# A modulation prologue in which every second unit is split into a high and a low part

## The reference

```python
sh1, sc1, g1, sh2, sc2, g2 = split(silu(c) @ mod_w[0] + mod_b[0])          # 1024 -> 6 x 1024
csh1, csc1, ...            = split(silu(c_ctx) @ mod_w[0] + mod_b[0])
n_lat = rmsnorm(x, norm1_g[0]) * (1 + sc1) + sh1
n_ctx = rmsnorm(ctx, norm1_g[0]) * (1 + csc1) + csh1
q, k, v, xr, gr = split(n_lat @ w_in);  kc, vc, xc = parts of n_ctx @ w_in
```

## Time and profile before

| | |
|---|---|
| median of 3 runs | 2468.14 us |
| profiled execution | 2467.85 us, its span 2466.0 us |
| TensorE busy | 98% of the span |
| first matmul of the projection | 57.85 us after the span's start |
| modulation units on TensorE | 15.55 to 53.7 us |
| granted clock of TensorE, whole span | 0.995 |

### The profile page before, as it was taken

How to read it: one execution, slowest core, us unless ns; L and a number is a source line. 1 busy time by engine, 2 the same in 40 slices (tenths; PEclk the granted TensorE clock), 3 DMA queues, 4 the chain that set the end, 5 groups by cost and what they waited for, 6 DMA issues and landing times.

```text
span 2466.0 us, 29290 instructions
## 1 busy us (share of the span) xinstructions
PE 2416.2 (98%) x11158; PEld 1982.8 (80%) x11158; DVE 1109.6 (45%) x1427; ACT 513.3 (21%) x816; POOL 1052.4 (43%) x507
## 2 busy tenths in 40 slices
PE   8999999989999999999999999999999999999998
PEld 3888878878788888888887888887788888888886
DVE  5677848844634443422224644346422222222224
ACT  4544438851200000000002200002200000000003
POOL 3333347888533334444334243553344433333340
PEclk9999999999999999999999999999999999999999
DMA  9444465533332233211111111111111111111111
GB/s 307 151 149 158 148 165 99 104 112 103 120 119 101 95 119 119 85 48 46 43 51 43 35 52 43 55 53 46 52 52 51 43 44 49 43 43 50 51 43 69
DMA packets 223343, 207.08 MB, mean 84 GB/s; under 512 B 40135, under 2 KB 193443, under 8 KB 222755
## 3 DMA queue, kind: packets, MB, share of 16 engines
q1 hardware_dynamic: 216787, 187.16, 25.8%
q10 hardware_dynamic: 5904, 16.78, 1.9%
q0 software_dynamic: 576, 2.10, 0.2%
HBM read 185.73 MB, written 20.28 MB: 84 GB/s over the span
## 4 chain that ended last, share of the span: by engine, by line
PE 92%; DVE 4%; ACT 2%; issue 1%; POOL 0%; DMA 0%; SPq 0%; DVEq 0%; POOLq 0%; ACTq 0%
PE bank L798 28%; PE bank L800 28%; PE bank L799 28%; PE bank L911 1%; DVE probs L1976 1%; PE bank L1041 1%; PE bank L1067 1%; PE bank L1066 1%; DVE bank L1663 1%; PE bank L1028 1%; PE bank L832 1%; ACT probs L1502 1%; PE bank L1029 1%; DVE act_lo L1669 1%; DMA mod_ring<-in_mod_w 0%
## 5 line engine op out<-in xcount | busy, mean ns | idle before, releaser
L628 POOL TENSOR_TENSOR w_hi<-raw,ones 128x1024 fp32r<-128x1024 f32 x184 | 359.6, 1954 | 1185.0 <-PE bank L800 1132.0
L798 PE MATMUL bank<-act_hi,w_hi 128*128 128x512 f32 x2160 | 844.7, 391 | 8.5 <-DVE hid_f L2026 5.8
L799 PE MATMUL bank<-act_hi,w_lo 128*128 128x512 f32 x2168 | 846.5, 390 | 0.0
L800 PE MATMUL bank<-act_lo,w_hi 128*128 128x512 f32 x2160 | 843.2, 390 | 0.0
L798 PEld LDWEIGHTS bank<-act_hi,w_hi 128*128 128x128 f32 x2160 | 406.9, 188 | 93.8 <-DVE hid_f L2026 6.6
L799 PEld LDWEIGHTS bank<-act_hi,w_lo 128*128 128x128 f32 x2168 | 408.7, 189 | 84.6
L800 PEld LDWEIGHTS bank<-act_lo,w_hi 128*128 128x128 f32 x2160 | 406.9, 188 | 85.5
L631 POOL TENSOR_TENSOR w_lo<-raw,w_hi 128x1024 fp32r<-128x1024 f32 x184 | 468.4, 2546 | 14.5
L1686 DVE SCALAR_TENSOR_TENSOR h<-bank,mods,h 128x512 f32<-128x512 f32 x432 | 319.0, 748 | 243.7 <-PE bank L800 243.0
L2026 DVE TENSOR_TENSOR hid_f<-silu_g,bank 128x512 f32<-128x512 f32 x86 | 59.1, 687 | 689.7 <-PE bank L800 687.4
L798 PE MATMUL bank<-hid_hi,w_hi 128*128 128x512 f32 x704 | 276.0, 392 | 1.6 <-DVE hid_lo L2033 1.4
(11 more groups left out here) (232 smaller groups left out, 2328.5 us busy)
## 6 DMA issues: line engine op xcount, KB each, us to landing
raw<-in_ffn_w_gu SPq DMA_DIRECT2D x88, 512.0 KB, 3.8
mod_in_f<-in_mod_w SPq DMA_DIRECT2D x48, 512.0 KB, 4.7
raw<-in_ffn_w_down SPq DMA_DIRECT2D x44, 512.0 KB, 3.6
mod_in_p<-in_mod_w SPq DMA_DIRECT2D x32, 512.0 KB, 6.6
raw<-in_o_w_in SPq DMA_DIRECT2D x24, 512.0 KB, 3.7
raw<-in_e_w_in SPq DMA_DIRECT2D x20, 512.0 KB, 5.1
mod_ring<-in_mod_w SPq DMA_DIRECT2D x16, 512.0 KB, 9.4
raw<-in_e_w_out SPq DMA_DIRECT2D x16, 512.0 KB, 3.6
```

The source lines that it names most:

```text
L628: nc.gpsimd.tensor_tensor(w_hi, raw[:, parity, :], ones[:, 0:1].to_broadcast([P, UNIT]), ALU.mult).then_inc(s_hi, 1)
L798: pe.matmul(dst, w_hi, x_hi, start=first, stop=False)
L799: pe.matmul(dst, w_lo, x_hi, start=False, stop=False)
L800: return pe.matmul(dst, w_hi, x_lo, start=False, stop=last)
```

## The change

- Odd modulation units (1, 3, ..., 15) are no longer multiplied in fp32. ACT rounds each to fp32r (`mod_high`) into slot 2 or 3 of `w_hi4`, POOL subtracts (`mod_low`) into the same slot of `w_lo4`, and TensorE multiplies both parts with `cond_r`.
- `cond_r` has four columns: the high parts of silu(c) and silu(c_ctx), and their low parts. The even units use `cond4`, with two columns of zeros. The sums therefore have four rows; the transposes have four columns, and VectorE adds the two extra ones.
- Unit 0 comes after row tile 5 (before: 4), so five units stand among the tiles, and the spreads come after unit 8 (before: 9).
- Weight units 2 and 3 are loaded behind all modulation units, and POOL makes the weight splits behind all eight `mod_low`.
- ACT has the roundings of units 1 and 3 behind the squares of tiles 6 and 8, that of 5 behind the root, those of 7 and 9 behind Exp, those of 11, 13 and 15 behind the mod_row copies of sh1.

```diff
+        def mod_slot(u):
+            return 2 + u // 2 % 2
...
@@ sync
             for u in range(8, 2 * FT):
                 load_first_mod(u)
-                if u in (11, 13):
-                    j = (u - 7) // 2
-                    load_unit(j, j % 2, column_unit(w_in, order_p[j]))
+            for j in (2, 3):
+                load_unit(j, j % 2, column_unit(w_in, order_p[j]))
...
@@ gpsimd
+            nc.gpsimd.memset(cond4[:, :, 2:4], 0.0)
...
+            def mod_low(u):
+                pool.wait_ge(s_mhi, u // 2 + 1)
+                nc.gpsimd.tensor_tensor(w_lo4[:, mod_slot(u), :], mod_ring[:, u % 8, :], w_hi4[:, mod_slot(u), :],
+                                        ALU.subtract).then_inc(s_mlo, 1)
+
+            for u in range(1, 2 * FT, 2):
+                mod_low(u)
             for j in range(4):
-                split(j, j, j % 2)
+                split(j, j, j % 2, None if j < 2 else (s_modmm, 2 * FT))
...
@@ tensor
             def first_mod(u):
                 c, k = divmod(u, FT)
-                pe.wait_ge(s_mod[u % 8], 16 * (u // 8 + 1))
+                if u % 2:
+                    pe.wait_ge(s_mlo, u // 2 + 1)
+                else:
+                    pe.wait_ge(s_mod[u % 8], 16 * (u // 8 + 1))
                 for a in range(2):
-                    mm = pe.matmul(bank[0:2, 4 + 2 * c + a, :], cond[:, k, :], mod_ring[:, u % 8, a * HALF:(a + 1) * HALF],
-                                   start=(k == 0), stop=(k == FT - 1))
+                    dst, cols_ = bank[0:4, 4 + 2 * c + a, :], slice(a * HALF, (a + 1) * HALF)
+                    if u % 2:
+                        pe.matmul(dst, cond_r[:, k, :], w_hi4[:, mod_slot(u), cols_], start=False, stop=False)
+                        mm = pe.matmul(dst, cond_r[:, k, :], w_lo4[:, mod_slot(u), cols_], start=False, stop=(k == FT - 1))
+                    else:
+                        mm = pe.matmul(dst, cond4[:, k, :], mod_ring[:, u % 8, cols_], start=(k == 0), stop=False)
...
-                if tt >= 4:
-                    if tt == 4:
+                if tt >= 5:
+                    if tt == 5:
                         pe.wait_ge(s_cond, 2)
+                        pe.wait_ge(s_condl, 1)
                         pe.wait_ge(s_param, 2)
-                    first_mod(tt - 4)
+                    first_mod(tt - 5)
             pe.wait_ge(s_xp, TT + CT)
-            for u in range(TT + CT - 4, 2 * FT):
+            for u in range(TT + CT - 5, 2 * FT):
                 first_mod(u)
-                if u == 9:
+                if u == 8:
                     pe.wait_ge(s_rstd, 1)
...
@@ scalar
+            def mod_high(u):
+                act.wait_ge(s_mod[u % 8], 16 * (u // 8 + 1))
+                if u >= 4:
+                    act.wait_ge(s_modmm, u - 3)
+                nc.scalar.copy(w_hi4[:, mod_slot(u), :], mod_ring[:, u % 8, :]).then_inc(s_mhi, 1)
...
+                    act.wait_ge(s_cond, 2)
+                    nc.scalar.copy(cond_r[:, :, 0:2], cond4[:, :, 0:2]).then_inc(s_condh, 1)
+                    nc.scalar.copy(cond[:], cond4[:, :, 0:2]).then_inc(s_cond, 1)
...
+                if tt in (6, 8):
+                    mod_high(tt - 5)
...
+            mod_high(5)
             act.wait_ge(s_xinv, 1)
             act.wait_ge(s_turn, TT + CT)
...
+            mod_high(7)
+            mod_high(9)
             for c in range(2):
                 act.wait_ge(s_modmm, FT * (c + 1))
...
+                if c == 0:
+                    for u in (11, 13, 15):
+                        mod_high(u)
...
@@ vector
-                    V.tensor_tensor(dst[:, c, :], summed[:, :, j], mod_bias[:, c, :], ALU.add).then_inc(s_modset, 1)
+                    V.tensor_tensor(dst[:, c, :], summed[:, :, j], mod_bias[:, c, :], ALU.add).then_inc(s_modadd, 1)
+                dve.wait_ge(s_modadd, 2 * (c + 1))
+                for j, dst in enumerate((mods, mods_ctx)):
+                    V.tensor_tensor(dst[:, c, :], summed[:, :, 2 + j], dst[:, c, :], ALU.add).then_inc(s_modset, 1)
...
+                if tt == 4:
+                    dve.wait_ge(s_condh, 1)
+                    dve.wait_ge(s_cond, 3)
+                    V.tensor_tensor(cond_r[:, :, 2:4], cond4[:, :, 0:2], cond_r[:, :, 0:2], ALU.subtract).then_inc(s_condl, 1)
```

More of the change, by code:

```diff
@@ L153, in backbone @@
         ctx_t = at(72, "ctx_t", [P, FT, CTX])
-        mod_row = at(83, "mod_row", [2, 2, UNIT])
+        mod_row = at(83, "mod_row", [4, 2, UNIT])
         x_sq = at(92, "x_sq", [P, D])
@@ L158, in backbone @@
         b_rows = at(80.5, "b_rows", [96, P])
+        cond4 = at(81, "cond4", [P, FT, 4])
+        cond_r = at(81.25, "cond_r", [P, FT, 4], F32R)
         far_rows = at(96, "far_rows", [P, HEADS * NR * GRID * GRID // (4 * P)])
@@ L242, in backbone @@
         s_modrow_d = sem("mod_row_by_dve")
+        s_condh, s_condl, s_mhi, s_mlo, s_modadd = (sem("cond_hi"), sem("cond_lo"), sem("mod_unit_hi"), sem("mod_unit_lo"),
+                                                    sem("mod_bias_added"))
         s_mu = (sem("mod_unit_landed0"), sem("mod_unit_landed1"))
@@ L925, in mod_turn @@
                 for m in range(FT):
-                    mm = pe.transpose(bank[:, 3, 2 * (c * FT + m):2 * (c * FT + m) + 2], mod_row[:, c, m * P:(m + 1) * P],
-                                      ident[0:2, 0:2])
+                    mm = pe.transpose(bank[:, 3, 4 * (c * FT + m):4 * (c * FT + m) + 4], mod_row[:, c, m * P:(m + 1) * P],
+                                      ident[0:4, 0:4])
                 mm.then_inc(s_modt, 1)
@@ L1386, in _ @@
                     for j in range(2):
-                        nc.scalar.activation(cond[:, :, j], par[:, PAR["c"] + j * FT:PAR["c"] + (j + 1) * FT], ACT.Silu).then_inc(s_cond, 1)
+                        nc.scalar.activation(cond4[:, :, j], par[:, PAR["c"] + j * FT:PAR["c"] + (j + 1) * FT], ACT.Silu).then_inc(s_cond, 1)
+                    act.wait_ge(s_cond, 2)
+                    nc.scalar.copy(cond_r[:, :, 0:2], cond4[:, :, 0:2]).then_inc(s_condh, 1)
+                    nc.scalar.copy(cond[:], cond4[:, :, 0:2]).then_inc(s_cond, 1)
                 act.wait_ge(s_x[tt], 16)
@@ L1404, in _ @@
                 for a in range(2 - c):
-                    nc.scalar.copy(mod_row[:, c, a * HALF:(a + 1) * HALF], bank[0:2, 4 + 2 * c + a, :]).then_inc(s_modrow, 1)
+                    nc.scalar.copy(mod_row[:, c, a * HALF:(a + 1) * HALF], bank[0:4, 4 + 2 * c + a, :]).then_inc(s_modrow, 1)
+                if c == 0:
+                    for u in (11, 13, 15):
+                        mod_high(u)
             act.wait_ge(s_xp, TT)
@@ L1782, in mod_first @@
                 dve.wait_ge(s_modt, c + 1)
-                summed = bank[:, 3, 2 * c * FT:2 * (c + 1) * FT].rearrange("p (m j) -> p m j", j=2)
+                summed = bank[:, 3, 4 * c * FT:4 * (c + 1) * FT].rearrange("p (m j) -> p m j", j=4)
                 for j, dst in enumerate((mods, mods_ctx)):
-                    V.tensor_tensor(dst[:, c, :], summed[:, :, j], mod_bias[:, c, :], ALU.add).then_inc(s_modset, 1)
+                    V.tensor_tensor(dst[:, c, :], summed[:, :, j], mod_bias[:, c, :], ALU.add).then_inc(s_modadd, 1)
+                dve.wait_ge(s_modadd, 2 * (c + 1))
+                for j, dst in enumerate((mods, mods_ctx)):
+                    V.tensor_tensor(dst[:, c, :], summed[:, :, 2 + j], dst[:, c, :], ALU.add).then_inc(s_modset, 1)
             for s, credits in ((s_conv, 1), (s_lru, 1), (s_macc, 2), (s_hup, 2),
@@ L1816, in _ @@
             dve.wait_ge(s_modmm, 2 * FT)
-            V.tensor_copy(mod_row[:, 1, HALF:UNIT], bank[0:2, 7, :]).then_inc(s_modrow_d, 1)
+            V.tensor_copy(mod_row[:, 1, HALF:UNIT], bank[0:4, 7, :]).then_inc(s_modrow_d, 1)
             mod_first(1)
```

## The result

The changed kernel took 2481.54 us (median of 4 runs, 2480.77 to 2482.45); the kernel before, run beside it on the same chip, 2467.94 (2467.33 to 2468.61). The ratio is 1.0056, 95% interval 1.0045 to 1.0068: 13.6 us slower. The profiled execution took 2480.77 us, its span is 2478.9.

What follows compares the result with a forecast made beforehand. TensorE, busy 98% of the span, was taken to bound the kernel, so the prologue's end decides. Terms A to D, 2.8 + 2.35 + 8 + 1 = 14.2 us, on 2467.85 gave 2482 us, range 2473 to 2489.

Steps and rivals of the forecast that it cites:

- term A: Modulation prologue: the wait for unit 7 and the low clock delay x_rms, so gains come 2.8 us later.
- Term B: Around VectorE's gains: the low part of unit 1 falls between the two gains operations, +2.35 us.
- Term C: Modulation of rows: splits of weight units 2 and 3 collide with VectorE's first eight act_lo, +8 us (0 to 8.5).
- Term D: Projection: TensorE, fed in pieces, starts its second group at the low clock, +1 us (0 to 2.5).
- Part 1: Odd units on TensorE: four fp32r matmuls of 0.23 us replace four fp32 records, 6.6 us less work.
- Part 2: Waits of odd units in the prologue: landing, ACT's rounding, POOL's subtraction; TensorE stands 5.5 us before unit 7.
- Part 3: Weight splits moved later on POOL: they and VectorE's SBUF-only operations exclude each other; x_rms is free.
- Edits costed at nothing: Copies of cond and a small subtraction are hidden; SP's moved queue has 10 us cover for gates and for weights.
- Nothing waits: Rival: the 6.6 us come in full as unit 7's low part is ready by 32.7; 2461 us, chance 0.07.
- The wait at unit 7 alone: Rival: only term A, without VectorE and POOL excluding each other; 2470.7 us, chance 0.09.
- SP's queue too late: Rival: the strip is slower by more than its cover, 5 us more, 2487 us; chance 0.05.
- Half the collisions: Rival: weight units 2 and 3 land late behind the spill, fewer collisions; 2473 to 2477 us, chance 0.17.

Runs made afterwards that it cites:

- experiment 1: The changed kernel with ACT rounding modulation unit 7 before its wait for VectorE's reciprocal; 2474.88 us, ratio 1.0028.
- 11: The changed kernel with weight units 2 and 3 split behind all act_lo, ACT's sp wait moved, far rows and memsets brought forward; 2473.92 us.
- 6: The changed kernel with unit 7 rounded earlier, weight unit 0 split behind it, weight units 2 and 3 behind all act_lo, ACT's sp wait moved; 2471.46 us.
- pair 3 and 4: The changed kernel with all 16 modulation units in fp32; splits of weight units 2 and 3 behind the modulation matmuls, 2470.52 us, or free, 2465.95 us.
- experiment 2: The changed kernel with POOL splitting weight units 2 and 3 only behind all 24 act_lo; 2482.11 us, ratio 1.0059.
- 5: The changed kernel with weight units 2 and 3 split behind all act_lo and ACT's sp wait moved to just before first use; 2480.47 us.
- experiment 8: The changed kernel with ACT issuing the 4 MB spill of h after the first eight act_hi; 2481.77 us, ratio 1.0055.
- experiment 7: The changed kernel with only units 9, 11, 13, 15 split, weight unit 0 first, weight units 2 and 3 behind all act_lo, sp wait moved; 2469.78 us.

## Why the prediction was right

The forecast was 2482.0 in a range of 2473 to 2489; it came to 2481.5. The two causes are the two that it named, and each was taken away by itself (experiments 1 and 11: 6.3 and 7.1 us, together 13.4 of 13.6; they were not taken away together with all eight units kept, except in 6, which had the late queue). Inside the second, one place and one wait were wrong, and part of the closeness of the total is luck: on the span, term A came to 3.9 us where 2.8 was said, B to 2.2 for 2.35, C to 5.0 for 8 and D to 1.4 for 1, so C was 3 us too large and A and D 1.5 us too small.

**Part 1, the work removed.** Right. Steps of 0.23 us as taken from the earlier trace rows; the even units and the small additions on VectorE cost what they did.

**Part 2 and term A (+2.8, bounds +0.6 and +4).** The chain was right link by link: x_diag 30.53, table load 33.58, unit 7's rounding behind it on ACT, POOL's low part, TensorE's stall of 4.7 us (5.5 was said), the low clock behind it. ACT's row in the changed kernel, to be laid beside the earlier trace rows:

```profile
30.53 3.03 ACT L1431 ACTIVATE x_diag<-ident,x_std 128x128 f32<-128x128 f32 x10 [3.90 <-DVE x_std L1848]
33.58 1.28 ACT L1434 ACT_TABLE_LOAD   x1
```

The term measured +3.9, the upper bound: all of unit 8 ran at the low clock (3.57 us for four records, twice 1.8), so that the spread began at 43.8 and not at 42.8. The mis-sized part is the length of that low stretch, and it changes from one execution to the next: experiments 2, 5, 8 and 11 have the same program up to there, and their gains came at 58.73, 56.83, 58.20 and 60.08 us, 1.4 to 4.6 us behind the kernel before; unit 8 took 3.07, 2.55 and 3.58 us in the first three. So +2.8 was a fair middle, and +3.9 is one profile's. Unit 0 at 2.4 GHz with a longer stall behind it (3.14 us) was the alternative that the text gave, at no other cost.

**Part 3.** That VectorE and POOL exclude each other was right, and shown by the pair 3 and 4, where nothing else differs. The rows give it as an exchange one for one: from 71 us on, four of VectorE's operations each end 0.3 to 0.6 us behind one of POOL's four (two act_lo end at 76.49, POOL's second operation at 75.95). x_rms, which has one input in PSUM, loses nothing: 16 take 11.52 us beside POOL's low parts and splits (11.51 in the earlier trace rows). By the rule in the Trainium skill ("SBUF — State Buffer", Who interferes with whom) a VectorE operation with one SBUF input, outside the two-port modes, does not meet GpSimd, and one with two does. The trace agrees: 11.52 us beside POOL for x_rms, and 5.20 in place of 1.40 for two act_lo. Shared bandwidth would not make 2.2 us of a 128x8 operation.

**Term B (+2.35).** The sum was right, +2.2 (6.05 less 3.86), its place was not: the low part of unit 1 (59.70 to 62.04) met the two `scaled` behind the gains, and did not fall between the two gains operations.

**Term C (+8, bounds 0 and 8.5).** VectorE lost 7.2 us (its last ctx_lo is 13.24 us late, 6.05 of it from before), so the price held. The step that failed is "landing 5 us and more after issue ... are split while VectorE makes the first eight act_lo". The first of them landed 13.1 us after issue, and the collision fell on the second eight. The bound of 0 for that case was wrong: it took the splits behind the eighth act_lo to be free, and TensorE needed the second eight as well as the chain behind them. Of VectorE's 7.2 us TensorE felt 2.9 (78.5 to 81.3) and 2.1 (95.4 to 97.5). The second is a link that the prediction did not have: the chain of 23 small operations, ACT's wait for them and the bank that ACT frees, with 0.8 us of cover before. Experiment 8 shows what the forecast's own placing would have given: the same total.

**Term D (+1).** The low clock came in a later group and cost 1.7 us (4.0 x 0.42), inside its bounds of 0 to 2.5. The first group's low stretch was shorter than before, 10 matmuls and not 12, which gives back 0.3: the second group starts at 71.64 in place of 65.88, 5.76 us late and not 6.05. On the span: 3.9 + 2.2 - 0.3 + 2.9 + 1.7 + 2.1 = 12.5 of the 12.9 us; the remaining 0.4 comes after the sixth group and has no single place.

**Edits costed at nothing.** SP's queue brought no stall: its cover was to be 10 us and TensorE's delay of 13 us lengthened it. The condition was stated ("gone if terms A to D were zero") and experiments 5 to 7 are that case, though by another way: not the transfers came too late, but POOL's splits moved onto VectorE's recurrence. There it cost 5.1 us (experiment 7); that the text gave 4 to 5 is chance, as its cause was another.

**The rivals.** "Nothing waits" was decided at unit 7's low part, which came at 38.4 and not by 32.7. "The wait at unit 7 alone" fell with the rows of act_lo (5.20 us for two) and with experiment 1, which took that wait away and was still 7.3 us over the kernel before. "SP's queue too late" fell with the rows of SP's work: no stall of TensorE came from it. "Half the collisions" had its condition met (the weights did land late behind the spill) and its price wrong, for the reason under term C. It had 0.17; given what the trace of before shows of the chain of small operations, its time should have been close to the forecast's.

## What to carry to other kernels

Before work is moved onto an idle GpSimd, write down for each stretch what VectorE does then: if it works in SBUF alone, each GpSimd operation that met it held it up here by nearly its own length, 1.7 to 2.2 us for an operation of 0.17, however small VectorE's was; beside operations that read one input from PSUM it was free. When such work is moved, look at what moves behind it in its own queue and in the DMA queue that waits for it, since a lead on TensorE brings other collisions a round later. And add to a stall of TensorE the low clock that follows it. Counted by the same matmuls in the kernel before, it cost a further 1.7 us behind a stall of 2.1 us (experiment 1), 2.6 behind 2.4 (7), 1.7 behind 2.7 (the changed kernel), 2.8 behind 4.4 (6), 2.1 behind 4.7 (5) and 1.7 behind 7.0 (2); behind the 1.95 us at 97.53 in the changed kernel there was none.

## What the runs showed that I had not expected

- A load of 512 KB took 13.1 us behind a store of 4 MB from another queue, and 3.7 us without it (experiment 8); the earlier trace rows had 5.0.
- VectorE's operations on 128x8 take 1.7 to 2.2 us each beside GpSimd's splits and 0.17 alone (experiment 2): a chain of 23 tiny operations, of which four met a split, became what TensorE waited for.
- A stall of 2.4 us cost 5.1: the granted clock was 0.50 for 5 us behind it (experiment 7).
- Six of the larger stalls of TensorE stand in its rows as "issue" (97.53 in the changed kernel, and one each in experiments 1, 2, 5, 6 and 7). The end of another engine's row beside the start of TensorE's tells what it was: VectorE's xc_lo ends at 165.63 and TensorE starts at 165.73 in experiment 7, at 175.90 and 176.00 in 5, at 168.52 and 168.61 in 6; ACT's copy ends at 97.30 and TensorE starts at 97.40 in 2, at 97.43 and 97.53 in the changed kernel, at 91.63 and 91.73 in 1.
